# Expert routing moved from a stage of its own into the output stage of a two-layer DiT trunk

## The chip, the cores and the metric

The kernel runs on one core of one Trainium2 chip. The metric is the device time of one execution in microseconds, a median over runs. All data is fp32. In the rows, PE is TensorE, PEld its weight loads, DVE VectorE, ACT ScalarE, POOL GpSimd, SP SyncE; a name with a q behind it is that engine's sequencer.

## What is computed

Each of two layers mixes 512 latent and 256 context tokens (the second layer only the latent ones), then runs a mixture of experts. The part at hand:

```
h = h + gate * (mixed @ w_out)                      # output projection, gated residual
u = rmsnorm(h, norm2_g) * (1 + scale) + shift       # 1024 wide
lg = u @ w_router_g (8 groups); le = u @ w_router_e (64 experts)
group = argmax(lg + b); two experts in the group = top-2 of (le + b)
weight = softmax(lg)[group] * softmax(le of the two)
y[token] += weight * (silu(u @ w_gate[e]) * (u @ w_up[e])) @ w_down[e]
```

Each of 64 experts has w_gate and w_up of 1024 x 256 and w_down of 256 x 1024: 3 MB, all read once per layer.

## The kernel before

The core works on 128-token tiles: NT = 6 in layer 0 (two streams, latent and context, with modulations of their own, NS = 2), NT = 4 in layer 1 (NS = 1). Each stage is a block of instruction streams, one per engine, tied by semaphores; a stage begins when all engines have ended the one before. Within DVE, `Chain` (line 155) puts a wait between each instruction and the next.

**Output stage** (`out_stage`, line 2114). SP loads the gate, gain and shift rows, then calls `then`: six router loads (`router_loads`, line 2350: two weight parts, two biases, a triangle, counters), then the weights of experts 0 to 2 into ring slots 0 to 2. For each tile PE runs the output product, two halves of eight fp32 matmuls of 512 columns (each is two instructions on the engine, so 16 a half); DVE gates it and adds it to the residual (lines 2202, 2204); ACT squares and sums (2182); DVE and ACT make 1/rms r (2206, 2184, 169 to 172); DVE makes the normed rows utok = h*r*gain + shift (2213, 2215); SP stores them to `rows_in`, from which experts gather. PE transposes the rows of the tile before (2147), ACT copies them out of PSUM (2188), PE multiplies them with the router weights (2155, 72 columns), DVE keeps the logits (2196). Transposes and logits of tile j-1 stand in PE's order behind the product of tile j; those of the last tile stand alone at the end.

**Router stage** (`router_stage`, line 2361). SP loads experts 3 to 5 at its start. DVE selects group and experts for all tiles at once in some 50 chained instructions, PE ranks the tokens of each expert with a triangle matmul and builds, for each expert, a list of up to 64 rows.

**Expert stage** (`moe_stage`, line 2554). The 64 experts pass through a ring of RU = 6 weight slots. For expert j GpSimd gathers rows by an indirect DMA (2636) into one of three buffers that it zeroes first (2632), PE transposes them (2533), ACT copies (2714), PE computes gate and up (2517, 32 instructions), ACT and DVE the gated product, PE transposes it and multiplies with w_down (2525), DVE (in layer 0 ACT as well) copies, GpSimd scatters (2643). SP loads the gate and up part of expert j+6 when `gu_done` of expert j is up, its down part when `down_done` is. PE opens with 28 dummy products (`keep_warm`, line 175; each is two instructions). DVE opens with `late_slots` (2767), the lists of experts with over 64 rows.

**Memory.** Slots 0 to 2 lie on the left of SBUF. Slots 3 to 5 lie on the right, over the mixed activations and w_out (slots 4 and 5) and over buffers of the output stage (slot 3).

## Time and profile before

| | us |
|---|---|
| runs (3) | 2730.29, 2730.78, 2731.94; median 2730.78 |
| profiled execution | 2734.9; span from first to last instruction 2733.1 |
| mean granted TensorE clock | 0.973 |
| PE busy | 2496.2 (91% of the span) |
| DVE, ACT, POOL busy | 1048.2, 573.7, 659.2 |

The profiled execution is 4.1 us above the median of the runs, and 1.8 us of it lie outside its span. Busy shares are averages over stages with different limits, so the profile is read stage by stage. The output stage of layer 0 begins at 900.9 us and its expert stage at 1037.0; in layer 1 these are 2100.0 and 2195.5.

### The profile page before, as it was taken

How to read it: one execution, taken by the hardware profiler on the slowest of the kernel's cores; microseconds unless marked ns; L12 is line 12 of the kernel's file. 1: busy time of each engine (PE TensorE's matmuls, PEld its weight loads, DVE VectorE, ACT ScalarE, POOL GpSimd, SP SyncE). 2: the span in 40 equal slices, each digit the busy share in tenths (PEclk: the TensorE clock that was granted, in tenths of full speed). 3: DMA queues.
4: the chain of work that ended last, by engine and by line, in shares of the span. 5: the costliest groups of instructions: out<-in, count | busy, mean ns of one | idle time of the engine just before them, and what ended most of it. 6: DMA issues, size and time to landing. Idle time of an engine off the chain costs nothing. (4 is left out here: it accounts for less than half of the span.)

```text
span 2733.1 us, 35245 instructions
## 1 busy us (share of the span) xinstructions
PE 2496.2 (91%) x13186; PEld 1551.0 (57%) x13186; DVE 1048.2 (38%) x1936; ACT 573.7 (21%) x1152; POOL 659.2 (24%) x604
## 2 busy tenths in 40 slices
PE   7998989899999989998888889989999999988887
PEld 2445666555555456555555568655787565555553
DVE  5565477444222234221111165844422443222222
ACT  4352111243111111221111141024310111111111
POOL 0003211366122002222221222036531022222221
PEclk9999999999999999999999999989999999999999
DMA  9883130020122518999999913012035389999996
GB/s 354 309 303 111 53 118 18 7 59 1 47 69 85 207 79 334 389 401 401 401 392 384 358 62 113 31 31 53 24 93 167 155 343 397 390 401 407 401 405 255
DMA packets 209099, 588.26 MB, mean 215 GB/s; under 512 B 47376, under 2 KB 109115, under 8 KB 158684
## 3 DMA queue, kind: packets, MB, share of 16 engines
q1 hardware_dynamic: 185925, 557.10, 54.4%
q0 software_dynamic: 22400, 29.42, 3.3%
q8 instruction: 68, 1.11, 0.2%
q14 instruction: 43, 0.35, 0.0%
q10 hardware_dynamic: 663, 0.27, 0.0%
HBM read 581.31 MB, written 51.51 MB: 232 GB/s over the span
## 5 line engine op out<-in xcount | busy, mean ns | idle before, releaser
L2517 PE MATMUL ps<-w,moe_xt 128*64 128x256 f32 x4096 | 489.7, 393 | 93.2 <-DMA w<-in_w_up_e 91.0
L2517 PEld LDWEIGHTS ps<-w,moe_xt 128*64 128x64 f32 x4096 | 320.3, 141 | 218.0 <-issue 100.3
L2643 POOL DMA_INDIRECT rows_out<-moe_rows_out,table x128 | 118.4, 925 | 740.5 <-DVE moe_rows_out L2708 365.9
L2525 PE MATMUL ps<-w,moe_ht 128*64 128x512 f32 x1024 | 247.8, 605 | 2.3 <-issue 2.3
L2756 DVE TENSOR_TENSOR moe_gated<-ps,moe_gated 64x256 f32<-64x256 f32 x128 | 54.5, 425 | 497.8 <-ACT moe_gated L2727 497.8
L2727 ACT ACTIVATE moe_gated<-ps 64x256 f32<-64x256 f32 x128 | 48.2, 376 | 665.8 <-PE ps L2517 665.8
L1712 POOL TENSOR_SCALAR attn_p<-attn_p,attn_rs 128x768 f32<-128x768 f32 (+1 forms) x80 | 155.1, 1947 | 81.6 <-DVE attn_rs L1881 81.2
L2533 PEld LDWEIGHTS ps<-ident,moe_xg 64*128 64x128 f32 x1024 | 122.5, 200 | 57.5 <-issue 57.4
L2165 PE MATMUL ps<-w_out,mix 128*128 128x512 f32 x320 | 145.4, 615 | 7.0 <-PEq L150 7.0
L2533 PE MATMUL ps<-ident,moe_xg 64*128 64x64 f32 x1024 | 139.6, 277 | 8.2 <-DMA moe_xg<-rows_in,rows 8.0
L2742 DVE TENSOR_TENSOR moe_rows_out<-ps,moe_row_gate 64x512 f32<-64x512 f32 x128 | 88.0, 688 | 140.4 <-PE ps L2525 138.3
L2636 POOL DMA_INDIRECT moe_xg<-rows_in,rows x128 | 121.6, 950 | 44.2 <-issue 36.9
L2165 PEld LDWEIGHTS ps<-w_out,mix 128*128 128x128 f32 x320 | 62.4, 197 | 84.7 <-issue 84.7
L2525 PEld LDWEIGHTS ps<-w,moe_ht 128*64 128x64 f32 x1024 | 62.4, 136 | 84.2 <-issue 75.5
L2714 ACT ACTIVATE moe_xt<-ps 128x512 f32<-128x512 f32 x128 | 76.4, 597 | 107.8 <-PE ps L2533 107.8
L2533 PEld LDWEIGHTS ps<-ident,moe_gated 64*128 64x128 f32 x256 | 39.9, 203 | 103.6 <-issue 103.6
L2708 DVE COPY moe_rows_out<-ps 64x512 f32<-64x512 f32 x64 | 44.3, 693 | 133.4 <-PE ps L2525 133.4
L1976 POOL TENSOR_TENSOR mix<-merge_g 128x768 f32<-128x768 f32 (+1 forms) x16 | 24.6, 1535 | 261.0 <-DVE merge_g L2079 261.0
L1875 DVE TENSOR_REDUCE attn_nm<-ps 128x1 f32<-128x768 f32 (+1 forms) x80 | 68.0, 850 | 26.0 <-PE ps L1759 25.4
L1989 PE MATMUL ps<-yh,w_merge 128*128 128x384 f32 (+1 forms) x256 | 74.3, 445 | 1.6 <-PEq L150 1.6
L1989 PE MATMUL ps<-merge_t,w_merge 128*128 128x384 f32 (+1 forms) x256 | 74.1, 432 | 0.0
L2087 DVE TENSOR_TENSOR merge_g<-ps,merge_p 128x384 f32<-128x384 f32 (+1 forms) x16 | 7.9, 491 | 167.7 <-PE ps L1989 167.7
(415 smaller groups left out, 3924.7 us busy)
## 6 DMA issues: line engine op xcount, KB each, us to landing
w<-in_w_gate_e SPq DMA_DIRECT2D x128, 1024.0 KB, 25.6
w<-in_w_up_e SPq DMA_DIRECT2D x128, 1024.0 KB, 29.6
w<-in_w_down_e SPq DMA_DIRECT2D x128, 1024.0 KB, 29.4
prep_w<-in_w_ada SPq DMA_DIRECT2D x24, 2048.0 KB, 13.5
w_merge<-in_w_in SPq DMA_DIRECT2D x32, 512.0 KB, 5.4
y<-rows_out SPq DMA_DIRECT2D x20, 512.0 KB, 7.8
transfer<-prep_out POOLq DMA_DIRECT2D x8, 1024.0 KB, 6.4
h<-transfer SPq DMA_DIRECT2D x4, 2048.0 KB, 11.6
```

The lines of the kernel that those rows point to most:

```text
L1712: nc.gpsimd.tensor_scalar(p, p, s["rs"][:, u % 4:u % 4 + 1], None, ALU.mult).then_inc(s["norm_done"], 1)
L1875: nc.vector.tensor_reduce(s["nm"][:, u % 2:u % 2 + 1], scores_of(u), axis=AX.X, op=ALU.max, negate=True).then_inc(s["max_done"], 1)
L1989: ins = nc.tensor.matmul(m.ps[:, bank, 0:H], lhs[:, k], rhs[:, k], start=k == 0, stop=k == KH - 1)
L2165: last = nc.tensor.matmul(m.ps[:, 2 * (j % 2) + half], m.mix[:, c, tile * P:(tile + 1) * P], w[:, half, c], start=c == 0, stop=c == KC - 1)
L2517: last = nc.tensor.matmul(ps[k * SLOTS:(k + 1) * SLOTS, 0:DE], xt[:, c], wgu[:, k, c], start=c == 0, stop=c == KC - 1)
L2525: last = nc.tensor.matmul(ps[k * SLOTS:(k + 1) * SLOTS, 0:512], ht[:, c], wd[:, c, k * 512:(k + 1) * 512], start=c == 0, stop=c == 1)
L2533: last = nc.tensor.transpose(ps[:, c * SLOTS:(c + 1) * SLOTS], src.rearrange("p (q c) -> p c q", c=n)[:, c], ident[0:SLOTS, 0:SLOTS])
L2636: nc.gpsimd.indirect_dma_start(out=xg[:, j % GR], out_offset=None, in_=dram["u"], in_offset=bass.IndirectOffsetOnAxis(ap=m.rows[0:SLOTS, j ...
L2643: nc.gpsimd.indirect_dma_start(out=dram["y"], out_offset=bass.IndirectOffsetOnAxis(ap=m.table[0:SLOTS, j:j + 1], axis=0), in_=y[:, j % 2], ...
L2714: return nc.scalar.activation(out, in_, ACT.Copy)
L2742: return lambda out, in_: nc.vector.tensor_tensor(out, in_, s["row_gate"][half * SLOTS:(half + 1) * SLOTS], ALU.mult)
L2756: nc.vector.tensor_tensor(h[:, b % 2], m.ps[SLOTS:2 * SLOTS, b % 2, 0:DE], sg[SLOTS:2 * SLOTS, b % 2], ALU.mult).then_inc(s["h_done"], 1)
```

## The change

The router stage goes. Its work is done tile by tile inside the output stage:

- The product of each tile is handled in halves by DVE and ACT (`gate`, `square`), on buffers of 512 columns.
- PE transposes the **unnormed** residual, in halves (`turn`), and multiplies it with router weights that DVE has scaled with the gain. Logits are that product times r plus a constant row (shift @ router weights, plus bias), made once per stream by PE between the two halves of the first product (`constants`, 8 matmuls of 72 columns per stream).
- Transposes and logits of tile j-1 stand between the two halves of product j. DVE selects tile j-1 (`selection`, `weights_begun`) between the two halves of `gate(j)`, and after the second half runs `ranked(j-1)`, `root(j)`, `weights(j-1)`. PE's `rank` and `lists` stand behind each product.
- GpSimd makes the normed rows in three passes of 1024 columns over one buffer; ACT's queue stores them.
- SP loads slots 4 and 5 when the last product is done, and slot 3 at the start of the expert stage, ahead of everything else that SP issues there.
- For the last tile, selection, ranking, lists and weights follow at the end of the stage. The exponentials are taken per tile, with a dummy Sqrt behind each for ACT's function table.

The diff, cut (the constants of `constants` on DVE, `weights_begun`, `weights` and ACT's helpers are left out: the last three are 5, 6 and one to two instructions a tile):

```diff
-def out_stage(nc, m, l, dram, streams, early, picks, then):
+def out_stage(nc, m, l, dram, streams, early, picks, then, freed):
...
+            sp.wait_ge(s["mm_done"], 2 * NT)
+            freed(sp)
+            sp.wait_ge(s["u_out"], 16 * NT)
...
+            def product(j, half):
+                if j == 0:
+                    pe.wait_ge(loaded[half], 16)
+                if j >= 2:
+                    pe.wait_ge(s["prod_done"], 2 * (j - 2) + half + 1)
+                    if half:
+                        pe.wait_ge(s["slots_done"], j - 1)
+                tile = work[j][1]
+                for c in range(KC):
+                    last = nc.tensor.matmul(m.ps[:, 2 * (j % 2) + half], m.mix[:, c, tile * P:(tile + 1) * P], w[:, half, c],
+                                            start=c == 0, stop=c == KC - 1)
+                last.then_inc(s["mm_done"], 1)
+            def constants():
+                pe.wait_ge(picks["router_in"], ROUTER_LOADS * 16)
+                pe.wait_ge(s["spread"], NS)
+                for t in range(NS):
+                    for c in range(KC):
+                        last = nc.tensor.matmul(m.ps[:, 6, CONST + t * R:CONST + (t + 1) * R], spread[t][:, c], wr[:, c], start=c == 0, stop=c == KC - 1)
+                last.then_inc(s["const_done"], 1)
+            def rank(j):
+                pe.wait_ge(s["both_done"], j + 1)
+                if j >= 1:
+                    pe.wait_ge(s["slots_done"], j)
+                nc.tensor.matmul(m.ps[:, 2 * (j % 2) + 1, 0:NE], m.ones[:], s["before"][:, j % 2], start=True, stop=False)
+                nc.tensor.matmul(m.ps[:, 2 * (j % 2) + 1, 0:NE], triu[:], s["both"][:], start=False, stop=True).then_inc(s["rank_done"], 1)
+            def lists(j):
+                pe.wait_ge(s["slots_done"], j + 1)
+                for k in range(2):
+                    last = nc.tensor.matmul(m.ps[0:SLOTS, 7, 0:NE], s["slot"][:, k], s["tag"][:, k],
+                                            start=j == 0 and k == 0, stop=j == NT - 1 and k == 1)
+                last.then_inc(s["listed"], 1)
+            for j in range(NT):
+                product(j, 0)
+                if j == 0:
+                    constants()
+                else:
+                    turn(j - 1, 0)
+                    turn(j - 1, 1)
+                    logits(j - 1)
+                product(j, 1)
                 if j >= 2:
...
+                    lists(j - 2)
                 if j >= 1:
...
+                    rank(j - 1)
+            pe.wait_ge(s["prod_done"], 2 * (NT - 1))
+            turn(NT - 1, 0)
+            keep_warm(nc, m, 0, 2)
+            turn(NT - 1, 1)
+            keep_warm(nc, m, 0, 3)
+            logits(NT - 1)
+            lists(NT - 2)
+            keep_warm(nc, m, 0, 16)
+            rank(NT - 1)
+            pe.wait_ge(s["total_done"], 1)
+            nc.tensor.matmul(m.ps[:, 5, 0:NE], m.ones[:], s["before"][:, NT % 2], start=True, stop=True).then_inc(s["rank_done"], 1)
+            keep_warm(nc, m, 0, 2)
+            lists(NT - 1)
+            keep_warm(nc, m, 0, 8)
+            for j in range(NT):
+                if j >= 1:
+                    turned_out(j - 1, 0)
+                    turned_out(j - 1, 1)
+                square(j, 0)
+                if j >= 1:
+                    store(j - 1)
+                    exponentials(j - 1)
+                    nc.scalar.activation(s["table"][:, j:j + 1], m.ones[:, 0:1], ACT.Sqrt)
+                if j == NT - 1:
+                    turned_out(j, 0)
+                square(j, 1)
+                if j == NT - 1:
+                    turned_out(j, 1)
+                root(j)
+            nc.scalar.activation(s["table"][:, 0:1], m.ones[:, 0:1], ACT.Exp)
+            store(NT - 1)
+            exponentials(NT - 1)
+        @block.gpsimd
+        def _(pool):
+            pool.wait_ge(s["g_in"], 48 * NS)
+            pool.wait_ge(s["const_done"], 1)
+            for j, (t, tile) in enumerate(work):
+                pool.wait_ge(s["added"], 2 * j + 2)
+                if j >= 1:
+                    pool.wait_ge(s["u_out"], 16 * j)
+                nc.gpsimd.tensor_tensor(s["utok"][:], m.resid[:, tile], s["g"][:, t, 1], ALU.mult).then_inc(s["gained"], 1)
+                pool.wait_ge(s["gained"], j + 1)
+                pool.wait_ge(s["r_done"], j + 1)
+                nc.gpsimd.tensor_scalar(s["utok"][:], s["utok"][:], s["r"][:, j:j + 1], None, ALU.mult).then_inc(s["scaled"], 1)
+                pool.wait_ge(s["scaled"], j + 1)
+                nc.gpsimd.tensor_tensor(s["utok"][:], s["utok"][:], s["g"][:, t, 2], ALU.add).then_inc(s["utok_done"], 1)
+            def gate(j, half):
+                t, tile = work[j]
+                done = 2 * j + half
+                dve.wait_ge(s["mm_done"], done + 1)
+                if done:
+                    dve.wait_ge(s["added"], done)
+                nc.vector.tensor_tensor(s["t"][:], m.ps[:, 2 * (j % 2) + half], s["g"][:, t, 0, cols(half)], ALU.mult).then_inc(s["prod_done"], 1)
+                dve.wait_ge(s["prod_done"], done + 1)
+                nc.vector.tensor_tensor(m.resid[:, tile, cols(half)], m.resid[:, tile, cols(half)], s["t"][:], ALU.add).then_inc(s["added"], 1)
+            def root(j):
                 r, var, tmp = (s[name][:, j:j + 1] for name in ("r", "var", "tmp"))
...
+                dve.wait_ge(s["sq_done"], 2 * j + 2)
+                nc.vector.scalar_tensor_tensor(var, s["ss"][:, j, 0:1], EPS, s["ss"][:, j, 1:2], ALU.add, ALU.add).then_inc(s["var_done"], 1)
                 dve.wait_ge(s["root_done"], j + 1)
                 refined_rsqrt(nc, link, r, var, tmp)
...
+                dve.sem_inc(s["r_done"], 1)
+            def first_max(val, hot, k):
+                link(nc.vector.tensor_reduce(row(k), val, axis=AX.X, op=ALU.max))
+                link(nc.vector.scalar_tensor_tensor(s["c"][:], val, row(k), s["turn"][:], ALU.is_equal, ALU.mult))
+                link(nc.vector.tensor_reduce(row(k), s["c"][:], axis=AX.X, op=ALU.min))
+                link(nc.vector.tensor_scalar(hot, s["c"][:], row(k), None, ALU.is_equal))
+            def selection(j):
+                t, tile = work[j]
+                r, got = s["r"][:, j:j + 1], m.ps[:, 6, 0:R]
+                dve.wait_ge(s["lg_done"], j + 1)
+                link(nc.vector.scalar_tensor_tensor(s["lgb"][:], got, r, s["const"][:, t, 1], ALU.mult, ALU.add))
+                first_max(s["lgb"][:, 0:NG], s["hot_g"][:], 0)
+                by_group = s["lgb"][:, NG:R].rearrange("p (g j) -> p g j", g=NG)
+                big = s["big"][:, 0].rearrange("p (g j) -> p g j", g=NG)
+                link(nc.vector.tensor_tensor(big, by_group, over(s["hot_g"][:, :, None], NG, EG), ALU.mult))
+                link(nc.vector.tensor_reduce(s["val"][:], s["big"][:, 0].rearrange("p (g j) -> p j g", g=NG), axis=AX.X, op=ALU.add))
+                first_max(s["val"][:], s["hot"][:, 0], 1)
+                link(nc.vector.scalar_tensor_tensor(s["val"][:], s["hot"][:, 0], LOW, s["val"][:], ALU.mult, ALU.add))
+                first_max(s["val"][:], s["hot"][:, 1], 1)
+                for k in range(2):
+                    last = nc.vector.tensor_tensor(sel[:, k, j].rearrange("p (g j) -> p g j", g=NG), over(s["hot_g"][:, :, None], NG, EG),
+                                                   over(s["hot"][:, k, None, :], NG, EG), ALU.mult)
+                link(last)
+                nc.vector.tensor_tensor(s["both"][:], sel[:, 0, j], sel[:, 1, j], ALU.add).then_inc(s["both_done"], 1)
+                dve.wait_ge(s["both_done"], j + 1)
+                link_total = nc.vector.tensor_tensor(s["before"][:, (j + 1) % 2], s["before"][:, j % 2], s["both"][:], ALU.add)
+                if j == NT - 1:
+                    link_total.then_inc(s["total_done"], 1)
+                    dve.wait_ge(s["total_done"], 1)
+                else:
+                    link(link_total)
                 if j >= 1:
...
+                    dve.wait_ge(s["listed"], j)
+                for k in range(2):
+                    nc.vector.tensor_tensor(s["tag"][:, k], sel[:, k, j], over(iota[:, 90 + k * TT + j:91 + k * TT + j], NE), ALU.mult)
+                if j >= 1:
+                    dve.wait_ge(s["exps"], j)
+                nc.vector.scalar_tensor_tensor(s["lg"][:], got, r, s["const"][:, t, 0], ALU.mult, ALU.add).then_inc(s["lg_evac"], 1)
...
+            def ranked(j):
+                dve.wait_ge(s["rank_done"], j + 1)
+                for k in range(2):
+                    last = nc.vector.tensor_tensor(s["big"][:, k], sel[:, k, j], m.ps[:, 2 * (j % 2) + 1, 0:NE], ALU.mult)
+                link(last)
+                link(nc.vector.tensor_reduce(pos[:, :, j], s["big"][:], axis=AX.X, op=ALU.add))
+                for k in range(2):
+                    last = nc.vector.tensor_tensor(s["slot"][:, k], iota[:, 0:SLOTS], over(pos[:, k, j:j + 1], SLOTS), ALU.is_equal)
+                last.then_inc(s["slots_done"], 1)
...
+            for j in range(NT):
+                gate(j, 0)
+                if j >= 1:
+                    selection(j - 1)
+                    weights_begun(j - 1)
+                else:
+                    constants()
+                gate(j, 1)
+                if j >= 1:
+                    ranked(j - 1)
+                root(j)
+                if j >= 1:
+                    weights(j - 1)
+            selection(NT - 1)
+            weights_begun(NT - 1)
+            ranked(NT - 1)
+            dve.wait_ge(s["rank_done"], NT + 1)
+            nc.vector.tensor_copy(cnt[:], m.ps[:, 5, 0:NE])
+            dve.wait_ge(s["listed"], NT)
+            listed = m.ps[0:SLOTS, 7, 0:NE]
+            link(nc.vector.tensor_scalar(s["late"][:], listed, -float(TOK), -float(TOK), ALU.is_ge, ALU.mult))
+            nc.vector.scalar_tensor_tensor(m.rows[0:SLOTS, 0:NE], listed, float(NO_ROW), s["late"][:], ALU.add, ALU.add)
+            nc.vector.tensor_scalar_add(m.table[0:SLOTS, 0:NE], listed, float(NO_ROW))
+            weights(NT - 1)
...
-def router_stage(nc, m, l, streams, picks, then):
...
-def moe_stage(nc, m, l, a, dram, ring, homes, streams, picks, out):
+def moe_stage(nc, m, l, a, dram, ring, homes, streams, picks, first_loads, out):
...
+            first_loads(sp)
...
-EARLY_EXPERTS = 3
+EARLY_EXPERTS, FREED_EXPERTS = 3, 4
...
+            for b in range(FREED_EXPERTS, RU):
+                slot_at[b] = top - (RU - b) * SLOT * 4
+                slots[b] = nc.alloc_sbuf_tensor_at(f"early_w{l}_{b}", [P, SLOT], F32, offset=slot_at[b])[:]
+            out_stage(nc, m, l, dram, streams, out_early, picks, out_prefetch, lambda sp: first_round(sp, range(FREED_EXPERTS, RU)))
             late.close()
-            top = nc.sbuf_top
+            assert top == nc.sbuf_top
             for b in reversed(range(EARLY_EXPERTS, RU)):
+                at = slot_at[b]
                 ring_buffer(b, "right")
-            router_stage(nc, m, l, streams, picks, lambda sp: first_round(sp, range(EARLY_EXPERTS, RU)))
+                assert at in (None, slot_at[b])
         homes = blend_homes(nc, l, slot_at, base, top, out is not None)
-        moe_stage(nc, m, l, a, dram, (slots, gu_in, down_in), homes, streams, picks, out)
+        moe_stage(nc, m, l, a, dram, (slots, gu_in, down_in), homes, streams, picks, lambda sp: first_round(sp, range(EARLY_EXPERTS, FREED_EXPERTS)), out)
```

## Rows read from the trace of the kernel before

**Rows 1.** Windows of the expert stage of layer 0: us, busy (count) per engine, clock, DMA, GB/s

```profile
1040.00:1050.00 10.00, 9.20 (x80) 7.84 (x78) 9.58 (x18) 2.26 (x3) 4.98 (x6) 1.00 0.18 40
...
1160.00:1200.00 40.00, 40.00 (x292) 23.05 (x290) 8.46 (x18) 9.39 (x18) 10.30 (x12) 1.00 1.02 402
```

**Rows 2.** Timeline of PE, start of both expert stages: start us, us, instruction

```profile
1036.98 6.49 PE L178 MATMUL ps<-ident 128*128 128x128 f32 x56 [0.30 <-PEq L150]
...
1045.28 3.67 PE L2517 MATMUL ps<-w,moe_xt 128*64 128x256 f32 x32 [0.78 <-ACT moe_xt L2714]
...
2195.56 6.49 PE L178 MATMUL ps<-ident 128*128 128x128 f32 x56 [0.30 <-PEq L150]
2204.55 1.11 PE L2533 MATMUL ps<-ident,moe_xg 64*128 64x64 f32 x8 [2.50 <-DMA moe_xg<-rows_in,rows]
2206.44 6.26 PE L2517 MATMUL ps<-w,moe_xt 128*64 128x256 f32 x32 [0.78 <-ACT moe_xt L2714]
```

**Rows 3.** Timeline of PE, last products of the output stages, transposes and logits

```profile
989.22 13.95 PE L2165 MATMUL ps<-w_out,mix 128*128 128x512 f32 x32
...
1005.16 2.00 PE L2155 MATMUL ps<-pick_wr,out_ut 128*128 128x72 f32 x16 [1.11 <-ACT out_ut L2188]
...
2152.30 13.95 PE L2165 MATMUL ps<-w_out,mix 128*128 128x512 f32 x32
```

**Rows 4.** Windows of L2165 alone, first halves of the first products: columns as PE, PEld

```profile
900.91:909.90 8.99, 8.99 (x17) 3.88 (x18) 0.81 0.89 299
2100.00:2109.90 9.90, 9.90 (x17) 4.23 (x18) 0.70 0.84 218
```

**Rows 5.** Timeline of SP, last router load; then the landing times of L2358

```profile
913.96 0.43 SPq L2358 DMA_DIRECT2D pick_iota<-const_iota  x1
...
2107.57 0.43 SPq L2358 DMA_DIRECT2D pick_iota<-const_iota  x1
...
DMA to landing us min/median/max: 2.4/2.4/2.5
```

**Rows 6.** Groups of GpSimd by form, then one of DVE

```profile
L1712 POOL TENSOR_SCALAR attn_p<-attn_p,attn_rs 128x768 f32<-128x768 f32 x64 | 140.5, 2203 | 63.3 <-DVE attn_rs L1881 62.9
...
L1712 POOL TENSOR_SCALAR attn_p<-attn_p,attn_rs 128x256 f32<-128x256 f32 x16 | 14.7, 923 | 18.4 <-DVE attn_rs L1881 18.4
...
L1404 POOL TENSOR_TENSOR conv_u<-conv_u 128x1024 f32<-128x1024 f32 x5 | 11.8, 2360 | 39.6 <-DVE conv_u L1448 39.6
...
L2742 DVE TENSOR_TENSOR moe_rows_out<-ps,moe_row_gate 64x512 f32<-64x512 f32 x128 | 88.0, 688 | 140.4 <-PE ps L2525 138.3
```

**Rows 7.** Timelines of GpSimd and DVE in the merge stage of layer 1

```profile
2068.73 1.33 POOL L1968 TENSOR_TENSOR merge_s<-merge_s,w_merge 128x512 f32<-128x512 f32 x1
...
2068.86 1.48 DVE L2099 TENSOR_TENSOR merge_g<-merge_p 128x256 f32<-128x256 f32 x1
...
2087.18 0.43 DVE L2098 TENSOR_TENSOR merge_g<-merge_g,merge_p 128x256 f32<-128x256 f32 x1
```

**Rows 8.** Timeline of DVE, small operations of the output, router and expert stages

```profile
1025.05 0.22 DVE L2456 TENSOR_TENSOR route_before<-route_before,route_both 128x64 f32<-128x64 f32 x1
1041.05 0.17 DVE L2779 TENSOR_SCALAR moe_q<-pick_pos 128x12 f32<-128x12 f32 x1
1042.08 1.67 DVE L2784 TENSOR_SCALAR moe_q<-moe_q 128x12 f32<-128x12 f32 x1
```

**Rows 9.** Gathers: timeline of GpSimd, the chain's first gather, landing times of L2636

```profile
1038.97 1.05 POOL L2636 DMA_INDIRECT moe_xg<-rows_in,rows  x1 [0.88 <-POOL moe_xg L2632]
1042.74 0.98 POOL L2632 MEMSET moe_xg<- 64x1024 f32 x1
...
2197.48 6.94 DMA moe_xg<-rows_in,rows
...
DMA to landing us min/median/max: 2.3/7.1/8.4
```

**Rows 10.** Landing times of the row stores, L2136

```profile
DMA to landing us min/median/max: 2.6/2.6/15.8
```

289 lines of the change are left out of this document (102 added, 187 removed).

## The prediction

> **What bounds the kernel now.** I read the windows of the expert stages first. Early in the expert stage of layer 0 the DMA engines stand at a share of 0.18; after that they are full, 1.02 and about 400 GB/s [rows 1], in 40 us windows down to the stage's end, and the same in layer 1. There all six slots are full and nothing may load until PE has used slot 0. So an expert stage is a fixed stream of 58 experts' weights (the first six are in), and its end moves with the moment at which the first gate-and-up product ends; I call it G. G is 1045.28 + 3.67 = 1048.95 in layer 0 and 2212.70 in layer 1 [rows 2]. Everything after an expert stage is a chain, so a shift of G shifts the end one for one, in each layer. Loads moved ahead of G save no bytes behind it: the ring still holds six experts at G, before and after. What counts is when G comes.
>
> G has two parts: the stage's start M (1036.98 and 2195.56, where PE's dummies begin) and the way from M to G, 12.0 and 17.1 us [rows 2]. The second is longer since the first gather came when PE had been idle 2.5 us, and the 32 products behind it took 6.26 us instead of 3.67, the lower of TensorE's two levels, 1.2 against 2.4 GHz.
>
> **Part 1: when the last output product ends.** Before, at 989.22 + 13.95 = 1003.2 and 2166.2 [rows 3]. Added ahead of it:
>
> - *Constants wait for the router loads.* They now stand behind the first half product. That half ends at 909.9 and 2109.9 (its 17th instruction has begun there) [rows 4]. Of the six loads the last is issued at 913.96 and 2107.57 and lands 2.4 us on: 916.4 and 2110.0 [rows 5]. Before, PE needed them only two tiles later. SP's order is unchanged. Layer 0 stalls 6.5 us, layer 1 0.1.
> - *Clock.* The first halves take 9.0 and 9.9 us where 16 instructions at 0.43 are 6.9, at a granted clock of 0.81 and 0.70, after PE had stood 3 to 4 us between stages [rows 4]. The new stall is longer, so layer 0 pays such a loss again: 2.1 us by the nearer row, bounds 0 and 3.0.
> - *Constant matmuls*: 16 instructions are spaced over 1.85 us [rows 3]: 3.7 (two streams) and 1.85.
> - *One more round of transposes and logits ahead of the last product's end.* A round costs what lies from the end of a product to the end of the logits' spacing, 1005.16 + 1.85 less 1003.0 = 4.0 [rows 3]; in halves ACT's copy overlaps the second transposes, 3.7. Five of 3.7 less four of 4.0: 2.5; layer 1, three less two: 3.1.
> - *Ranks and lists*: four instructions each, 0.25; seven of them 1.7, layer 1 three, 0.7.
>
> Sums: 16.5 and 5.8 us; the last products end at 1019.7 and 2172.0.
>
> **Part 2: from there to M.** Here the question is GpSimd beside DVE. GpSimd takes 2.36 us for 1024 columns of a tensor_tensor; its tensor_scalar is 0.923 at 256 columns and 2.203 at 768, so 2.84 at 1024 [rows 6]. Three passes: 7.5 us a tile, most of it while DVE has work. The timeline shows what that does. A DVE tensor_tensor of 256 columns with both inputs in SBUF takes 0.43 us alone (L2098 at 2087.18). Its like, L2099, starts at 2068.86 and ends at 2070.34, 1.48 us: just behind GpSimd's operation that ends at 2070.06 [rows 7]. A tensor_scalar of 12 columns takes 0.17 and 1.67, the latter ending with GpSimd's memset at 1043.7 [rows 8, 9]. So DVE operations with two operands in SBUF, and tensor_scalars, stand until GpSimd's current operation ends, then one of them gets in before the next. Of the 23 instructions of `selection` 14 are of this kind, of the six of `weights` four.
>
> The last tile, in us from the end of its product. Small DVE operations cost 0.16 to 0.22 plus 0.03 of chain [rows 8], half-tile ones 0.69 [rows 6].
>
> - DVE comes late to it. A tile's round on DVE (1.4 gate, 9.5 along GpSimd's three passes as below, 0.4, 1.4 gate, 5.9 selection) is 18.6 to 19.5 against PE's 18.2; lateness builds up to 2.6 by the last tile.
> - Gate: 0.2 + 2 x 0.69: 1.6.
> - GpSimd multiplies, 2.4. DVE is held at the slot compare. Then slots, variance, ACT's Sqrt and the refinement give r, 1.6. GpSimd scales, 2.8, and adds, 2.4, while DVE gets one instruction of `weights` in between. With change-overs 9.5, and 0.4 for the rest of `weights`.
> - Selection, 23 instructions 4.8; `weights_begun` 1.1; `ranked` 1.1; PE's list 0.4; three row operations 0.7; `weights` 1.2: 9.3. PE's rank and the exponentials are covered by DVE's own chain.
> - Stage exit 0.75.
>
> Sum 24.2. Before, 33.8 and 29.4 lay between those points (1036.98 less 1003.2; 2195.56 less 2166.2), router stage included. M comes at 1043.9 and 2196.2: later by 6.9 in layer 0 and 0.6 in layer 1.
>
> The last row store goes out at about +14. Bounds of its landing: 2.6 and 15.8 [rows 10], the latter behind 9 MB on its own queue. Slots 4 and 5 are 6.3 MB from +0.3 on, at 400 GB/s done by +16 or 17, and the store is on another queue; it lands before +24 in any case. Cost nothing, covered by DVE's chain; if that chain were 7 us shorter the store would set the end of the stage.
>
> **Part 3: from M to G.** The first gather still goes out 2.0 us behind M (1038.97). In layer 0 it met almost no load, DMA being at 0.18 [rows 1], and PE's dummies, which end at 1043.5, covered it [rows 2]. Now slot 3's 3 MB leave at M and take 8 us. The gather under load: 6.94 in layer 1, median 7.1, alone 2.3 [rows 9]. I take 6.9, since layer 1 was this very case. PE's transposes and ACT's copy, 1.9, then 3.7 or 6.3 for the products: G is 14.5 to 17.1 behind M. I take 16.0: the dummies may themselves start at the lower clock, after PE's gaps of 2 to 5 us in the tail, and then last until the gather is there. Layer 0 +4.0, layer 1 -1.1. The same load delays the row_gate rows in layer 1 by 8 us; they are first needed about 17 us in, so they cost nothing.
>
> The Trainium skill, "DMA: Bandwidth & Descriptors", section on queues, rings and completion order, says that each DMA engine takes turns between its queues by packets. By that rule a gather, on a queue of its own, would at most double its lone time, to an estimated 5 us; the sum would be about 4 us less. The rows show 7 under load, and decide.
>
> **Sum.** 6.9 + 4.0 + 0.6 - 1.1 = +10.4 us. Against the profiled execution, 2734.9, that is 2745.3; against the median of the runs, 2730.8, it is 2741.2.
>
> **Rivals.**
>
> - *A. Small operands do not collide.* The row of a collision with GpSimd's arithmetic is 256 columns wide [rows 7]; if operands of 1 to 64 columns slip through, DVE's lateness and its waits vanish. Then r is ready at +5.5, the lists at about +16, the row store sets the end of the stage at +17 to +18: M moves +1.0 and -5.4. With part 3: -1.5, 2729.3. This ends not slower; the point from which it decides is a wait of DVE of under 1 us a tile. For it: no row of 8 columns beside a GpSimd tensor_tensor. Against: the 12-column row at 1.67 [rows 8]. 0.20. The Trainium skill, "SBUF — State Buffer", section "Who interferes with whom", speaks of an exclusive lock held for a whole instruction, whatever its size; by that rule A could not happen, and the sum would stay at +10.4.
> - *B. The gather is not held up by slot 3.* Then G stays at 12.0 behind M in both layers: +6.9 + 0.6 - 5.1 = +2.4, 2733.2. For it: the landing of 2.3. Against: layer 1. 0.13.
> - *C. PE is cold at M.* With DVE held 6 us, PE stands about 5 us in the tail before the last rank and again behind it. 56 dummy instructions at half speed are 13.0 instead of 6.49, then cold products: G 21 us behind M, +6.9 + 9 + 0.6 + 3.9 = +20, 2751. 0.12.
> - *D. A and B together*: the shortened end shows in full: +1.0 - 5.4 - 5.1 = -9.5, 2721.3. 0.04.
> - The forecast's own case, 2741.2, own range 2735 to 2748: 0.51.
>
> A measurement can tell about 0.2%, 5.5 us, from no change: the borders are 2725.3 and 2736.3. Slower: nearly all of the forecast's case, and C: 0.60. Faster: D and the lower tail of A: 0.10. Same: 0.30. The range goes from A's lower part to C's: 2725 to 2750.
>
> **What the profile would show.** A gap of PE of about 6.5 us near 910 in layer 0 ahead of the 72-column products, and none in layer 1. Small DVE instructions of 0.2 us drawn out to 2 or more beside GpSimd's passes, above all the slot compare and `weights`. DVE's first-half gate beginning only when GpSimd's add has ended. Last products ending near 1019.7 and 2172; the dummies of the expert stages near 1044 and 2196; DMA at 1.02 from some 20 us later to the end as before. The forecast is wrong if selection of the last tile starts within 8 us of the last product, if the 72-column products start before 915, or if the first gather lands within 5 us.

## The result and the profile after

The changed kernel takes 2747.35 us (median of four runs, 2745.42 to 2749.88) against 2731.36 for the kernel before, a ratio of 1.0058 with a 95% interval of 1.0041 to 1.0076: slower by 0.6%, more than the 0.2% that can be told. The forecast was 2741.2, range 2725 to 2750, slower. The profiled execution took 2746.75, 1.75 us of it outside its span of 2745.0.

The output stage of layer 0 began at 896.97 instead of 900.91. In the 14 traces of this case, whose kernels differ only behind that point, it begins between 894.8 and 900.9, so this is a difference between executions. All comparisons are therefore counted from the first product of each output stage. Even so the first half product differs between executions: in the seven kernels in which PE waits for the router loads as in the changed one, it takes 8.7 to 10.2 us in layer 0, and their P lies between 120.2 and 122.1. A difference of P below some 2 us is therefore not put down to an edit. P is the end of the last output product, M the first dummy of the expert stage, G the end of its first gate-and-up product, "rest" what lies from G to the next output stage (layer 0) or to the end of the span (layer 1).

| us | P | M - P | G - M | G | rest |
|---|---|---|---|---|---|
| before, layer 0 | 102.3 | 33.8 | 12.0 | 148.0 | 1051.1 |
| after, layer 0 | 122.1 | 22.8 | 19.3 | 164.1 | 1050.9 |
| before, layer 1 | 66.3 | 29.3 | 17.1 | 112.7 | 520.4 |
| after, layer 1 | 73.1 | 22.4 | 17.4 | 113.0 | 520.0 |

G moved by +16.1 and +0.3 (forecast +10.9 and -0.5), and the rest kept its length, so the shift passed to the end one for one. -3.9 at the start, +16.1, +0.3 and -0.6 in the rests make the +11.9 us between the spans. The end of the stream is as before [rows 1]:

```profile
1160.00:1200.00 40.00, 40.00 (x292) 22.91 (x290) 8.46 (x18) 9.37 (x18) 10.29 (x12) 1.00 1.02 402
```

Timeline of PE after the change, the start of both output stages (what answers to rows 4 and 5):

```profile
896.97 10.17 PE L2162 MATMUL ps<-w_out,mix 128*128 128x512 f32 x16 [4.03 <-PEq L150]
912.23 3.69 PE L2171 MATMUL ps<-pick_wr,out_ut 128*128 128x72 f32 x16 [5.09 <-DMA pick_iota<-const_iota]
915.72 3.62 PE L2171 MATMUL ps<-pick_wr,out_utok 128*128 128x72 f32 x16
919.13 16.19 PE L2162 MATMUL ps<-w_out,mix 128*128 128x512 f32 x32
...
2111.97 8.55 PE L2162 MATMUL ps<-w_out,mix 128*128 128x512 f32 x16 [2.96 <-PEq L150]
2122.42 2.00 PE L2171 MATMUL ps<-pick_wr,out_ut 128*128 128x72 f32 x16 [1.91 <-DMA pick_iota<-const_iota]
```

In layer 0 PE stands 5.1 us for the last router load. Behind that everything is slow: the two streams' constants are spaced over 6.9 us (3.5 at full clock, as a run below shows), and the next two halves take 16.19 instead of 13.95 [rows 3]. In layer 1 PE stands 1.9 us, and nothing behind it is slow.

Timelines of layer 0's tail after the change: DVE, then GpSimd, then PE (with layer 1's last rows).

```profile
1019.56 0.36 DVE L2378 TENSOR_TENSOR out_tag<-pick_sel,pick_iota 128x64 f32<-128x64 f32 x2 [2.10 <-PE ps L2203]
...
1021.13 0.69 DVE L2319 TENSOR_TENSOR out_t<-ps,out_g 128x512 f32<-128x512 f32 x1
...
1023.17 2.06 DVE L2411 TENSOR_TENSOR out_slot<-pick_iota,pick_pos 128x64 f32<-128x64 f32 x2
...
1026.86 0.81 DVE L2399 TENSOR_TENSOR out_row<-out_row 128x1 f32<-128x1 f32 x1
...
1027.90 0.16 DVE L2401 TENSOR_TENSOR out_row<-out_row 128x1 f32<-128x1 f32 x1
...
1028.23 0.28 DVE L2354 SCALAR_TENSOR_TENSOR out_lgb<-ps,out_r,out_const 128x72 f32<-128x72 f32 x1
...
1030.23 1.69 DVE L2346 SCALAR_TENSOR_TENSOR out_c<-out_val,out_row,out_turn 128x8 f32<-128x8 f32 x1
...
1039.37 0.23 DVE L2402 TENSOR_SCALAR weight<-out_ex,out_row 128x2 f32<-128x2 f32 x1
```

```profile
1022.63 2.38 POOL L2296 TENSOR_TENSOR out_utok<-resid,out_g 128x1024 f32<-128x1024 f32 x1 [9.18 <-DVE resid L2321]
1026.55 2.84 POOL L2299 TENSOR_SCALAR out_utok<-out_utok,out_r 128x1024 f32<-128x1024 f32 x1 [1.53 <-DVEq L2329]
1029.47 2.43 POOL L2301 TENSOR_TENSOR out_utok<-out_utok,out_g 128x1024 f32<-128x1024 f32 x1
```

```profile
1012.00 7.08 PE L2162 MATMUL ps<-w_out,mix 128*128 128x512 f32 x16
...
1037.77 3.78 PE L178 MATMUL ps<-ident 128*128 128x128 f32 x16
1041.85 7.09 PE L178 MATMUL ps<-ident 128*128 128x128 f32 x56 [0.30 <-PEq L150]
1052.89 1.12 PE L2620 MATMUL ps<-ident,moe_xg 64*128 64x64 f32 x8 [3.96 <-DMA moe_xg<-rows_in,rows]
1054.79 6.31 PE L2604 MATMUL ps<-w,moe_xt 128*64 128x256 f32 x32 [0.78 <-ACT moe_xt L2802]
...
2216.74 1.11 PE L2620 MATMUL ps<-ident,moe_xg 64*128 64x64 f32 x8 [2.70 <-DMA moe_xg<-rows_in,rows]
2218.63 6.36 PE L2604 MATMUL ps<-w,moe_xt 128*64 128x256 f32 x32 [0.78 <-ACT moe_xt L2802]
```

Four things are to be seen. DVE comes 2.1 us late to the last gate, and what it waited for was PE's list of an earlier tile (L2203), not GpSimd. The slot compare is held to 2.06 us, ending as GpSimd's multiplication does; during GpSimd's tensor_scalar (1026.55 to 1029.39) DVE gives up only 0.65 us at L2399, and L2401 runs in 0.16. DVE ends at 1039.6, but PE's eight dummies, at the low clock, last until 1041.55 and so set the end of the stage, 2 us later. And the gather, issued at 1044.13, lets PE go on at 1052.89, with 32 slow products behind it (6.31 against 3.67 [rows 2]).

### The profile page after: what moved, and what is told of

It reads as the page before. It is cut to its first block and busy times, and to the rows that moved or that the text cites. A ratio compares the mean times of both kernels' runs of the same rounds, so it can differ in the third digit from the quotient of the medians.

```text
span 2745.0 us, 35647 instructions
## 1 busy us (share of the span) xinstructions
PE 2503.8 (91%) x13150; PEld 1554.8 (57%) x13150; DVE 1102.7 (40%) x2222; ACT 603.7 (22%) x1244; POOL 735.9 (27%) x634
## 5 line engine op out<-in xcount | busy, mean ns | idle before, releaser
L2604 PE MATMUL ps<-w,moe_xt 128*64 128x256 f32 x2816 | 340.2, 396 | 63.0 <-DMA w<-in_w_up_e 60.8
L2604 PEld LDWEIGHTS ps<-w,moe_xt 128*64 128x64 f32 x2816 | 219.5, 142 | 153.1 <-issue 69.8
L2604 PE MATMUL ps<-early_w,moe_xt 128*64 128x256 f32 x1280 | 153.0, 393 | 26.2 <-DMA early_w<-in_w_up_e 26.2
L2612 PE MATMUL ps<-w,moe_ht 128*64 128x512 f32 x704 | 170.4, 604 | 2.3 <-issue 2.3
L2162 PE MATMUL ps<-w_out,mix 128*128 128x512 f32 x320 | 148.0, 618 | 7.0 <-PEq L150 7.0
L2604 PEld LDWEIGHTS ps<-early_w,moe_xt 128*64 128x64 f32 x1280 | 100.4, 141 | 64.7 <-issue 31.6
L2612 PE MATMUL ps<-early_w,moe_ht 128*64 128x512 f32 x320 | 77.5, 605 | 0.0
L2612 PEld LDWEIGHTS ps<-w,moe_ht 128*64 128x64 f32 x704 | 43.0, 136 | 58.6 <-issue 52.6
## 6 DMA issues: line engine op xcount, KB each, us to landing
w<-in_w_up_e SPq DMA_DIRECT2D x88, 1024.0 KB, 29.3
w<-in_w_down_e SPq DMA_DIRECT2D x88, 1024.0 KB, 29.3
```

Source lines behind the costliest of these rows:

```text
L2162: last = nc.tensor.matmul(m.ps[:, 2 * (j % 2) + half], m.mix[:, c, tile * P:(tile + 1) * P], w[:, half, c], start=c == 0, stop=c == KC - 1)
L2604: last = nc.tensor.matmul(ps[k * SLOTS:(k + 1) * SLOTS, 0:DE], xt[:, c], wgu[:, k, c], start=c == 0, stop=c == KC - 1)
L2612: last = nc.tensor.matmul(ps[k * SLOTS:(k + 1) * SLOTS, 0:512], ht[:, c], wd[:, c, k * 512:(k + 1) * 512], start=c == 0, stop=c == 1)
```

## The experiments

Each kernel is the changed kernel with the edit shown. The table first, P to rest as above, each layer's pair; then the edits. The runs of the kernel before beside them had medians of 2730.2 to 2731.2. The changed kernel's own interval is 1.0041 to 1.0076, and those of gather first (at its edge), rows on DVE, no last dummies, two tags and stall filled overlap it: what is said of these five rests on the traces, one each.

| kernel | P | M - P | G - M | rest | median us, ratio to before (95%) |
|---|---|---|---|---|---|
| constants later | 109.9, 72.5 | 22.8, 21.7 | 19.2, 16.3 | 1051.2, 520.0 | 2732.8, 1.0011 (1.0002 to 1.0020) |
| rows on DVE | 120.2, 75.9 | 20.6, 20.8 | 18.0, 16.4 | 1050.2, 520.3 | 2743.2, 1.0054 (1.0038 to 1.0069) |
| gather first | 121.1, 73.6 | 23.4, 22.2 | 12.3, 12.0 | 1053.1, 522.2 | 2738.9, 1.0033 (1.0022 to 1.0044) |
| no last dummies | 120.6, 73.5 | 21.6, 20.8 | 16.9, 19.0 | 1050.2, 522.2 | 2744.1, 1.0048 (1.0033 to 1.0063) |
| two tags | 122.0, 73.4 | 20.9, 20.8 | 18.4, 16.3 | 1050.5, 521.5 | 2744.0, 1.0047 (1.0032 to 1.0062) |
| slots 3 to 5 late | 120.5, 73.6 | 23.3, 22.2 | 18.4, 17.2 | 1057.2, 534.8 | 2768.3, 1.0141 (1.0126 to 1.0157) |
| the same, gate rows first | 122.1, 73.4 | 22.8, 22.3 | 18.9, 17.3 | 1054.9, 529.7 | 2759.1, 1.0106 (1.0090 to 1.0121) |
| stall filled | 120.8, 73.7 | 23.3, 22.2 | 17.6, 17.2 | 1050.8, 521.5 | 2745.8, 1.0052 (1.0037 to 1.0068) |
| four together | 109.9, 71.2 | 19.7, 19.5 | 13.7, 13.3 | 1050.0, 520.9 | 2717.5, 0.9955 (0.9941 to 0.9969) |
| four, rows on DVE | 111.2, 71.2 | 18.1, 18.1 | 13.5, 14.0 | 1049.9, 521.3 | 2719.2, 0.9961 (0.9947 to 0.9975) |
| four less one: dummies kept | 109.9, 72.5 | 20.8, 20.8 | 12.4, 12.6 | 1053.1, 520.7 | 2720.9, 0.9968 (0.9959 to 0.9977) |
| four, rows on DVE, 20 dummies | 111.1, 71.2 | 18.0, 18.0 | 11.6, 12.2 | 1051.7, 521.5 | 2717.5, 0.9952 (0.9939 to 0.9966) |

**Constants later.** On PE, and likewise on DVE behind the second gate:

```diff
                 product(j, 0)
-                if j == 0:
-                    constants()
...
                 product(j, 1)
+                if j == 0:
+                    constants()
```

> The constants (8 products of 72 columns per stream on PE, their spread on DVE) move behind the second half of the first output product; all else is the changed kernel. G is the end of the first gate-and-up product of an expert stage, counted from the first instruction of the output stage before it; the changed kernel has 164.1 us in layer 0 and 113.0 in layer 1. Theory: in the changed kernel PE stands 5.1 us for the router loads in layer 0 and then runs slow, so that the first products lose another 5.7 us; both go, G at 153 to 154 in layer 0, and 1.9 us earlier in layer 1, sum about -12 us, 2735. Rival 1, only the stall goes and the slow clock is lost anyway: -7 us. Rival 2, the stall only moves to the next wait of PE, since the loads were not the bound: 0.

Timeline of PE, the same place:

```profile
895.90 15.67 PE L2162 MATMUL ps<-w_out,mix 128*128 128x512 f32 x32 [4.03 <-PEq L150]
911.40 1.90 PE L2171 MATMUL ps<-pick_wr,out_ut 128*128 128x72 f32 x16
913.14 1.95 PE L2171 MATMUL ps<-pick_wr,out_utok 128*128 128x72 f32 x16
914.93 7.08 PE L2162 MATMUL ps<-w_out,mix 128*128 128x512 f32 x16
```

The stall and the low clock both go; G comes 12.3 and 2.5 us earlier, the median 14.5 us. Both rivals fall. Against the seven kernels that keep the wait (P 120.2 to 122.1), P of layer 0 is 10.3 to 12.2 us earlier. This one wait, placed one half product (7 us) too early, carried most of the change's loss.

**Stall filled.** Does the clock fall because of the stall?

```diff
+                    if NS > 1:
+                        keep_warm(nc, m, 4, 20)
                     constants()
```

> In layer 0 PE runs 20 dummy products (4.6 us at full clock) where it would stand and wait for the router loads ahead of the constants; otherwise the changed kernel. Theory, the stall of 5.1 us costs twice, once as itself and once as 5.7 us of low clock behind it: filled, the products behind it run at full clock (32 products' instructions in 13.95 us, the 32 of the constants in 3.7), G of layer 0 comes 4 to 6 us earlier, 2742. Rival, the low clock follows from the start of the stage and not from the stall, or the dummies run slow themselves and end after the loads have landed: no gain, up to 3 us slower.

```profile
904.36 4.63 PE L178 MATMUL ps<-ident 128*128 128x128 f32 x40
911.87 2.85 PE L2171 MATMUL ps<-pick_wr,out_ut 128*128 128x72 f32 x16 [2.88 <-DMA pick_iota<-const_iota]
914.52 3.62 PE L2171 MATMUL ps<-pick_wr,out_utok 128*128 128x72 f32 x16
```

The dummies covered 4.6 us, but 2.9 us of idling were left, since the loads landed 16.1 us into the stage instead of 15.3, and the clock fell all the same: 0.50 from 914 to 918, just behind the stall. The constants are spaced over 6.1 us and the next 32 product instructions take 14.80: 2.5 + 0.9 = 3.4 us of clock loss, where the changed kernel has 3.4 + 2.2 = 5.6. The theory's 4 to 6 us did not come: G comes 2.5 us earlier, 1.3 of it in P, and P, 120.8, lies within the 120.2 to 122.1 of the kernels that do not fill the stall.

Is the loss set by the length of the stall? In those seven kernels the stall is 5.1 to 6.6 us and the clock loss 4.3 to 5.6, and the three with the shorter stalls (5.1 to 5.3) have the larger losses (5.5 to 5.6). So the traces do not bear out that a longer stall costs more clock. What they do show is in layer 1, with the same wait: after stalls of 0.7 to 1.9 us, in seven kernels (this one among them, since it fills layer 0 alone), the clock stayed at full and the next two halves took 13.95; after the one of 3.45 us (rows on DVE, below) it fell. A full cover of the stall was not reached, and what it would give is open.

**Two tags.** The lists' tags get two buffers, so DVE waits one tile longer back:

```diff
-                if j >= 1:
-                    dve.wait_ge(s["listed"], j)
+                if j >= 2:
+                    dve.wait_ge(s["listed"], j - 1)
                 for k in range(2):
-                    nc.vector.tensor_tensor(s["tag"][:, k], sel[...
+                    nc.vector.tensor_tensor(s["tag"][:, j % 2, k], sel[...
```

> The buffer of tags from which PE makes the lists is doubled, so that DVE waits for the list of the tile before last and not of the last tile; otherwise the changed kernel. Theory, DVE's lateness at the last gate (2.1 us in layer 0, much the same in layer 1) comes from this wait, which PE's list, standing behind the product, ends: it goes, the last gate begins within 0.3 us of its product, and the expert stage starts 2 us earlier per layer, total -4, 2743. Rival, DVE is late because GpSimd's passes hold it: then the wait goes and the time comes back at the next instruction, 0.

DVE's waits in layer 0's output stage, the changed kernel: us in total, times, longest.

```profile
DVE out_tag L2378 <- PE ps L2203: 9.0, 4, 2.6
```

With two buffers the line is gone, and the timeline of DVE has

```profile
1022.67 0.69 DVE L2319 TENSOR_TENSOR out_t<-ps,out_g 128x512 f32<-128x512 f32 x1 [0.66 <-PE ps L2162]
...
1024.70 2.09 DVE L2411 TENSOR_TENSOR out_slot<-pick_iota,pick_pos 128x64 f32<-128x64 f32 x2
```

DVE now waits for the product at the last gate; M - P falls by 1.9 and 1.6. The lateness came from the tag wait, and the rival falls. The slot compare is still held, so GpSimd's hold is real, but another matter.

**Rows on DVE.** GpSimd's block goes; DVE makes the rows behind `root(j)`:

```diff
+                nc.vector.scalar_tensor_tensor(s["utok"][:], m.resid[:, tile], s["r"][:, j:j + 1], s["g"][:, t, 1], ALU.mult, ALU.mult)...
+                nc.vector.tensor_tensor(s["utok"][:], s["utok"][:], s["g"][:, t, 2], ALU.add)...
```

> GpSimd does nothing in the output stage; DVE makes the normed rows in two passes of 1024 columns right behind the root, from the changed kernel otherwise. Theory, GpSimd's passes hold up DVE's small operations: the slot compare of the last tile falls from 2.06 to 0.36 us, the others to 0.16 to 0.23, against 2.5 us of passes that DVE now has in each tile; the part from the last output product to the start of the expert stage (22.8 us in layer 0) becomes 21.5, total -2 to -3 us. Rival, the hold-ups cost nothing on the path: that part is 2.5 us longer per layer, +5 us, and DVE falls behind PE by up to 2.5 us more at the last tile.

```profile
1020.95 0.36 DVE L2404 TENSOR_TENSOR out_slot<-pick_iota,pick_pos 128x64 f32<-128x64 f32 x2
...
1023.71 1.28 DVE L2332 SCALAR_TENSOR_TENSOR out_utok<-resid,out_r,out_g 128x1024 f32<-128x1024 f32 x1 [0.16 <-DVE out_r L172]
1025.03 1.23 DVE L2334 TENSOR_TENSOR out_utok<-out_utok,out_g 128x1024 f32<-128x1024 f32 x1
```

The slot compare is back at 0.36. DVE's own 2.5 us are less than what GpSimd's passes took from it: M - P falls by 2.2 and 1.7. In layer 1 the gain is eaten by a later P (75.9 against 73.1). Timeline of PE there:

```profile
2116.24 3.69 PE L2171 MATMUL ps<-pick_wr,out_ut 128*128 128x72 f32 x16 [3.45 <-DMA pick_iota<-const_iota]
2119.73 14.97 PE L2162 MATMUL ps<-w_out,mix 128*128 128x512 f32 x32
```

The first half product took 7.1 us instead of 8.6, so PE stood 3.45 us for the router loads instead of 1.9, and the clock fell behind it (0.50 from 2116 to 2120): the constants took 3.69 instead of 2.00, the next two halves 14.97 instead of 13.95. That is the 2.8 us. It is once more the wait that the constants cause, and not a price of the rows on DVE.

**Gather first.**

```diff
-            first_loads(sp)
             if gated_rows:
...
+            sp.wait_ge(gathered[0], 16)
+            first_loads(sp)
```

> SP waits for the first gather of the expert stage to land before it loads slot 3 (the row gate's rows go out first); otherwise the changed kernel. Theory, slot 3's load is what delays the gather: it lands about 2.5 us after its issue instead of 8 to 9, PE's dummies cover it, the first gate-and-up product runs at full clock, and its end comes 12 us behind the stage's first dummy instead of 19.3 and 17.4: -7.1 us in layer 0, -5.3 in layer 1, 2735. Rival 1, the gather is delayed by something else (slots 4 and 5, the row store, its own 64 rows): landing stays at 7 to 9 us, and slot 3 comes later still, total 0 to +2. Rival 2, gather early but expert 3's weights late: then the product of expert 3 stands for its slot, and of the 12 us half or less arrives.

Timeline of PE, layer 0; then of SP:

```profile
1041.68 6.49 PE L178 MATMUL ps<-ident 128*128 128x128 f32 x56 [0.30 <-PEq L150]
1048.44 1.06 PE L2620 MATMUL ps<-ident,moe_xg 64*128 64x64 f32 x8 [0.27 <-DMA moe_xg<-rows_in,rows]
1050.28 3.67 PE L2604 MATMUL ps<-w,moe_xt 128*64 128x256 f32 x32 [0.78 <-ACT moe_xt L2803]
```

```profile
1048.32 0.33 SPq L2627 DMA_DIRECT2D w<-in_w_gate_e  x1
...
1053.98 0.33 SPq L2627 DMA_DIRECT2D w<-in_w_gate_e  x1
```

The gather lands 4.4 us after its issue at 1043.96 instead of 8.8, and G - M is 12.3 and 12.0. So slot 3's load did delay it, and rival 1 falls. (In layer 1 the edit also puts the row-gate rows ahead of slot 3; layer 0 has none.) But both rests grew by 2.2 us, and of the 12.6 us by which G came earlier in the two layers 8.5 arrived. The reading for layer 0: slot 3 is asked for at 1048.32 and needs about 8 us (an estimate: 3.1 MB at the 400 GB/s of rows 1), to 1056, while G is at 1053.95; the first load behind G then queues for 2 us. Rival 2 had half or less arriving, by a stand of PE for expert 3's weights: two thirds arrived, and PE's waits between 1040 and 1100 name no weights. **The stream begins at the later of two moments, G and the end of the first loads.** This is inferred here; the next runs test it. Two limits of the estimate: the trace records the last part of slot 3 as landed at 1059.46, 11.1 us behind the first issue, so the 8 us stand for the time that the queue is taken up, not for the landing; and in layer 1 the rests of kernels in which slot 3 is early lie between 520.0 and 522.2, so that the 522.2 there shows nothing.

**Slots 3 to 5 late.**

```diff
-            sp.wait_ge(s["mm_done"], 2 * NT)
-            freed(sp)
```

> Slots 3, 4 and 5 all load at the start of the expert stage; nothing loads at the last output product. Otherwise the changed kernel. Theory, the expert stage is a stream that cannot begin before the first gate-and-up product has ended (G) nor before the ring's first loads are through: 9.4 MB at 400 GB/s are 24 us from the stage's start, and G comes at 17 to 19, so the stream begins 5 to 7 us later per layer: +10 to +14 us, 2758 to 2761. Rival, loading slots 4 and 5 early is worth nothing, since the ring holds six experts at G in any case and the queue is never empty: 0.

By the rule, 24 us from the first issue at 1040.03 end at 1064, 5.6 behind G at 1058.5; the rest of layer 0 grew by 6.3. Layer 1 lost 14.8, more than forecast. DVE's waits there say why:

```profile
DVE moe_gated L2842 <- DMA moe_row_gate<-mod_rows: 17.9, 1, 17.9
```

PE stood 11.7 us behind it, until 2241.44. The row-gate rows stand behind the three slots on SP's queue. A second kernel issues them ahead:

> Slots 3, 4 and 5 all load at the start of the expert stage, but in layer 1 the two row-gate rows go ahead of them on SP's queue. Theory, with the slots ahead of them these rows landed so late that DVE waited 17.9 us and PE 11.7 us for them in layer 1; with the rows ahead that wait goes and layer 1 loses what layer 0 loses, about 6 us instead of 14.8: 2760. Rival, the loss of layer 1 is that of the three slots themselves: 2768.

2759.05: the wait is gone from the list. Layer 0 loses 4.0 us this time and layer 1 9.7; by the rule its slots, issued from 2213.91 on, end at 2238 or later, 8 behind G at 2230.1. Both growths of layer 0 (6.3 and 4.0) and that of layer 1 lie within 2 us of the rule. So the early loading of slots 4 and 5 is worth some 12 us (2759.05 against 2747.35); this I had not priced apart.

**No last dummies.**

```diff
             lists(NT - 1)
-            keep_warm(nc, m, 0, 8)
```

> The eight dummy products that PE runs behind the last list of the output stage go; otherwise the changed kernel. Theory, in both layers they run at the low clock (3.78 and 3.68 us) and end 2 us behind DVE's last instruction, so they set the end of the stage: the expert stage begins 2.0 us earlier per layer. What of it arrives: at most -4 us, 2743; if PE is then colder through the dummies of the expert stage, these last longer but still end before the gather lands, so nothing is lost. Rival, the dummies keep the clock up: without them the first products of the expert stage run slower, and the total is 0 or above.

```profile
1042.87 8.68 PE L178 MATMUL ps<-ident 128*128 128x128 f32 x56 [2.08 <-PEq L150]
```

M comes 1.2 and 1.6 us earlier; the expert stage's dummies are colder, that is more of them run at the lower clock (8.68 and 8.28 us instead of 7.09 and 6.49). The median fell 3.2 us, which the runs do not tell from none, and the layers do not follow the forecast: in layer 0 G comes 5.1 us earlier, but 1.6 of it is in P, and 2.3 behind M, where the gather let PE go on sooner (7.5 us behind its issue) and the products took 5.2; in layer 1 the gather let PE go on only 11.5 us behind M instead of 9.2, and G did not move. What the edit is worth alone stays open.

**Four together**: constants later, gather first, no last dummies, two tags.

> Four edits of the changed kernel together: constants behind the second half of the first product, the gather before slot 3's load, no dummies behind the last list, two tag buffers. If each takes away a stretch of the path of its own, the sum is -12 (constants) -12 (gather) -4 (dummies) -4 (tags) = -32 us at most, 2715; with the dummies no longer keeping the clock and the tail's row store nearer to the end I take 2718 to 2724, which is 0.3 to 0.5% faster than the kernel before. Rival, the stream of the weights is the bound in another way (slot 3 late, DMA idle at the start): over 2730, no faster than the kernel before.

> The four edits together, and the normed rows on DVE, with GpSimd idle in the output stage. Theory, the tail is DVE's chain, and GpSimd costs it more than two passes of its own: 1 to 3 us faster than the four edits alone. Rival, with the tag wait gone DVE's own 2.5 us a tile become lateness at the last gate: 2 to 6 us slower than the four edits alone.

2717.5 us, just below the 2718 to 2724 expected, and 0.45% faster than the kernel before. From SP's timeline: slot 3 is asked for at 1032.88, so by the estimate of 8 us its load ends at 1041, and G is at 1041.3. By the rule nothing queues, and the rest is 1050.0. The windows of the two kernels show the hole that went (the changed kernel, then this one; the second to last column is the DMA share):

```profile
1040.00:1050.00 10.00, 8.64 (x64) 8.19 (x62) 7.63 (x19) 0.00 (x0) 5.26 (x6) 0.85 0.72 274
1050.00:1060.00 10.00, 6.33 (x34) 4.24 (x36) 5.34 (x9) 1.88 (x2) 1.74 (x2) 0.67 0.23 74
```

```profile
1036.00:1046.00 10.00, 8.86 (x78) 6.99 (x79) 5.86 (x11) 2.85 (x4) 2.68 (x2) 1.00 1.02 367
1046.00:1056.00 10.00, 10.00 (x74) 5.69 (x70) 1.84 (x4) 2.54 (x5) 1.88 (x2) 1.00 1.01 421
```

In the changed kernel the DMA share is 0.23 from 1050 to 1060, up to G at 1061.1: slot 3's load has landed at 1053.7, all slots are full, and PE waits for the gather and then runs slow products. Here the DMA engines are full from 1036 on.

One more bound shows in this run. In layer 1 DVE ends at 2181.10, but M is at 2182.06, where the three other kernels without the last dummies have 0.32 us between the two, in both layers. The last row store, issued at 2173.44, lands at 2181.61, and SP ends its part of the stage with the wait for it: it now sets the end, at a cost of some 0.6 us. In layer 0 M is 1.17 us behind DVE, which would fit the same, but the trace has no landing for that store.

With the rows on DVE as well, M - P is 1.6 and 1.4 us shorter, in part since the store goes out earlier and lands before DVE's end (2178.18 and 2179.77 in layer 1). The median, 2719.2, is not told apart from 2717.5, and the 1 to 3 us expected are not seen in it. In layer 0 G gains only 0.5: P is 1.3 us later, all of it in the first 32 product instructions (17.02 against 15.67 us), on which the edit has no hold.

The four edits again, with the dummies of the output stage put back:

> The four edits together without the third of them: the eight dummy products behind the last list stay. Theory, without them the stage starts 1.3 to 2 us earlier per layer, but PE is cold there and its dummies in the expert stage last 8 us instead of 6.5, beyond the landing of the gather, so removing them gave next to nothing: this kernel is within 2 us of the four together (2717.5). Rival, each removed stretch counts in full: 4 us slower than the four together.

2720.9, 3.4 us slower than the four, with overlapping intervals of the two ratios. My theory said at most 2, the rival 4; the number is nearer to the rival, but the traces do not give it to the dummies. In layer 0 G is the same (143.1 and 143.2), and the loss is in the rest (1053.1 against 1050.0). Slot 3 is asked for at 1032.23, G is at 1037.86: by the estimate its load ends 2.4 us behind G. Without the dummies it is asked for 2.7 us earlier (134.8 against 137.5 from the stage's start): 1.1 by M, and 1.5 since the gather landed 3.0 us after its issue instead of 4.5, a difference whose cause is open. In layer 1 G itself comes 1.9 us later, 1.3 of it in P, where the first 32 product instructions took 16.91 us against 15.67. The dummies themselves cost 1.1 and 1.3 us of M - P, and 1.3 and 0.7 come back in G - M, as the theory had it.

The last kernel has the four edits, the rows on DVE, and 20 in `keep_warm(nc, m, 7, 28)` of the expert stage:

> The four edits and the rows on DVE, with 20 dummies instead of 28 at the start of the expert stage. Theory, the stream of weights begins at the later of two moments, the end of the first gate-and-up product (G) and the end of slot 3's load (8 us behind the landing of the gather). In the kernel with 28 dummies the two stand within 1 us of each other. With 20 dummies the first product ends 2 us earlier, but the slot's load does not, so of 2 us per layer hardly any reaches the end: total within 2 us of 2719. Rival, the end goes with G alone: 4 us faster, 2715.

G comes 2.0 and 1.8 us earlier. In layer 0 1.8 of it are given back in the rest, as the rule says; in layer 1 0.2. The median fell 1.7 us, with overlapping intervals. By the rule the slot's load ends 1.5 and 0.8 us behind G. Half of G's gain arrived, so theory and rival each hold in one layer, on differences that are small for one trace each.

## Why the prediction was right, and where it was not

The sign and the mechanism held: G decides, the rest is constant, and the last product comes later by more than the tail gets shorter. The total was 5.6 us short (+16.0 measured, with an interval of +11.2 to +20.8; +10.4 forecast): 2747.35 is inside my range, by less than 3 us, and my +10.4 is just below the interval. G of layer 0 has 5.2 of it: 3.3 in P and 3.3 in G - M, less 1.4 in the tail; layer 1 has 0.8.

- **Part 1, the clock.** The mis-sized term. I took 2.1 us for the low clock behind the stall, bounds 0 and 3.0, from the loss in the first half product [rows 4]. Measured: 3.4 in the constants and 2.2 in the products, 5.6; in the seven kernels with this wait, 4.3 to 5.6, above my upper bound in all of them. Those rows bounded it badly, since the loss outlives one half. From the trace, the granted clock was 0.50 from 912 to 920 and 0.55 from 920 to 924.
- **The stall**: 5.1 instead of 6.5 in layer 0, 1.9 instead of 0.1 in layer 1. The loads landed 15.3 us into the stage, as rows 5 have it, but the first half varied (10.2 instead of 9.0; 8.6 instead of 9.9). I had no term for that: it gave P 1.2 us in layer 0 and took 1.4 in layer 1, which is chance. I had named a start of the 72-column products before 915 as a sign against me; they started at 912.23, in a stage that itself began 3.9 us earlier, so an absolute time was the wrong test. The constants' 3.7 us are 3.5 (911.40 to 914.93) in the run that has them later.
- **The other terms of Part 1**, an extra round and lists, were 4.2 and 3.8; what is left of P's shift is 19.8 - 5.1 - 5.6 - 3.5 - 1.2 (first half) = 4.4, and 4.5 in layer 1. Near enough.
- **Part 2** summed to 24.2 and measured 22.8 and 22.4: that it came so near is luck, since its errors cancel. The lateness of 2.6 was 2.1, but from a wait that I had not listed: `tag` of tile j-1 waits for the list of tile j-2, which PE issues behind a whole product. The step that failed is that I did not look up what stands ahead of that list in PE's queue. GpSimd's chain holds DVE less than I said: selection began 9.2 us behind P, not 14.1, since only its two tensor_tensors hold DVE to their end, and GpSimd stood 1.5 us for r. From selection's start to DVE's end took 11.4 instead of 9.3, 1.5 of that being L2346 held by the add. Then the cold dummies, 2 us that I had at nothing. The row store I had right: in layer 0 it landed at 1040.11, 21.0 us behind P and ahead of M.
- My own test in Part 2 (selection begins over 8 us behind P) held at 9.2, narrowly.
- **Part 3**: 19.3 and 17.4 instead of 16.0. The gather took 8.8 and 6.9 us instead of 6.9, and the products were slow in both layers (6.3). The run with the gather first shows that slot 3's load is the cause.

The Trainium skill, "DMA: Bandwidth & Descriptors", section on queues, rings and completion order, has each engine take turns between its queues by packets; worked out from that, the gather would have at most doubled. In layer 0 the traces do not speak against it: 4.4 us with the gather first, 8.8 with slot 3's load ahead. In layer 1 they do: 2.6 and 6.9.

**The rivals.** A: DVE's small operations do collide with GpSimd (2.06 and 1.69 us, against 0.36 and 0.23), so A fell, though it was nearer than I thought, as one of the three passes lets them through. B and D fell with the gather. C in part: PE was cold (at the lower clock) at M, but its 56 dummy instructions took 7.09 and 6.48, not 13; what cost was the idling behind them, of 4.0 and 2.7 us, and the slow products after it.

## What to carry to other kernels

When work is moved forward in a queue, look up when its inputs landed before; an engine that waits for them early pays the wait and then, where the wait is long enough for the clock to fall, the low clock behind it; here the second (4.3 to 5.6 us) was about as large as the first (5.1 to 6.6). In a kernel with a stream of weights behind a start-up, compute two moments, the first release of a buffer and the end of the first loads, and change whichever is later; in the layer 0 traces shortening the other gave next to nothing. A load that nobody needs yet should not start ahead of the small transfer on which everybody waits, but must follow it at once. And before an effect of 1 or 2 us is given to an edit, compare a stretch of the traces that the edit can't touch: here the first products alone differ by as much.
